# Fourteen of the dot products by GpSimd and ScalarE, more dots ahead of the gates, sixteen V rows added inside U

## The reference

```
h = rmsnorm(x) @ w_in                # 1024 x 2400
x = x + concat(four kinds of attention over h) @ w_out
x = x + peer(rmsnorm(x))
```

```
act = gelu(einsum('td,thkd->thk', h, u_tab[idx]))
out = einsum('thk,thkd->td', gate * act, v_tab[idx])   # gate: softmax of the 16 best scores
```

## Time and profile before

| | |
|---|---|
| median of 3 runs | 1641.34 us (1639.16 to 1643.42) |
| profiled execution | 1639.23 us, its span 1637.4 us |
| TensorE busy | 1593.9 us (97%) |
| VectorE busy | 1065.6 us (65%) |
| ScalarE busy | 543.6 us (33%) |
| GpSimd busy | 686.8 us (42%) |
| DMA | 525.77 MB, mean 321 GB/s |

### The profile page before, as it was taken

How to read it: one execution, slowest core, us unless ns; L and a number is a source line. 1 busy time by engine, 2 the same in 40 slices (tenths; PEclk the granted TensorE clock), 3 DMA queues, 4 the chain that set the end, 5 groups by cost and what they waited for, 6 DMA issues and landing times.

```text
span 1637.4 us, 31846 instructions
## 1 busy us (share of the span) xinstructions
PE 1593.9 (97%) x11548; PEld 1547.6 (95%) x11548; DVE 1065.6 (65%) x2517; ACT 543.6 (33%) x1424; POOL 686.8 (42%) x556
## 2 busy tenths in 40 slices
PE   7999999999999899999999999999999999999998
PEld 6888999999999899999988889999999999999998
DVE  4784799688886643343357847896888866544443
ACT  5775522655553000000056755216555540000000
POOL 6516614555553432233256156144545535333331
PEclk9999999999999999999999999999999999999999
DMA  9026288999999999999930262798999999999996
GB/s 356 14 100 248 91 302 330 338 410 410 409 409 361 389 410 408 408 407 408 407 135 1 104 257 91 282 336 313 411 409 409 409 372 380 410 410 409 409 410 272
DMA packets 141942, 525.77 MB, mean 321 GB/s; under 512 B 16160, under 2 KB 19744, under 8 KB 139424
## 3 DMA queue, kind: packets, MB, share of 16 engines
q1 hardware_dynamic: 86336, 322.57, 50.5%
q0 software_dynamic: 55520, 202.14, 31.5%
HBM read 523.60 MB, written 1.05 MB: 320 GB/s over the span
## 4 chain that ended last, share of the span: by engine, by line
PE 82%; DMA 10%; DVE 3%; ACT 2%; issue 1%; POOL 1%; SPq 0%; DVEq 0%; ACTq 0%; POOLq 0%
PE ps L617 81%; DMA ring<-in_peer_v 6%; DMA nat<-in_peer_v 3%; PE ps L614 2%; ACT grid L297 0%; DVE grid L1400 0%; DVE negmax L1404 0%; DMA x<-in_x 0%; ACT grid L969 0%; DVE x L1458 0%; ACT grid L1068 0%; ACT wh L1005 0%; POOL wl L586 0%; DVE grid L1453 0%; ACT grid L955 0%
## 5 line engine op out<-in xcount | busy, mean ns | idle before, releaser
L617 PE MATMUL ps<-grid,ring 128*128 128x160 f32 (+1 forms) x3712 | 525.6, 300 | 11.2 <-DMA ring<-in_peer_v 10.2
L617 PE MATMUL ps<-grid,nat 128*128 128x160 f32 (+1 forms) x3712 | 526.0, 300 | 6.4 <-DMA nat<-in_peer_v 4.9
L617 PEld LDWEIGHTS ps<-grid,ring 128*128 128x128 f32 x3712 | 508.9, 190 | 16.5 <-issue 16.3
L617 PEld LDWEIGHTS ps<-grid,nat 128*128 128x128 f32 x3712 | 508.9, 190 | 12.4 <-issue 12.0
L1682 DVE SCALAR_TENSOR_TENSOR grid<-grid,amount 128x1024 f32<-128x1024 f32 x96 | 123.3, 1285 | 157.6 <-DMA grid<-in_peer_v,lists 156.8
L1682 DVE SCALAR_TENSOR_TENSOR grid<-gath_a,amount,grid 128x1024 f32<-128x1024 f32 x94 | 120.7, 1285 | 141.4 <-DMA gath_a<-in_peer_v,lists 140.0
L599 POOL DMA_INDIRECT gath_a<-in_u_rows,lists x96 | 130.8, 1363 | 178.8 <-DVE dots L1651 124.0
L599 POOL DMA_INDIRECT gath_a<-in_peer_v,lists x96 | 107.5, 1120 | 224.4 <-PE ps L617 122.3
L579 POOL TENSOR_TENSOR wl<-grid,wh 128x512 fp32r<-128x512 f32 (+2 forms) x128 | 142.6, 1141 | 118.7 <-ACT wh L1005 97.0
L599 POOL DMA_INDIRECT grid<-in_peer_v,lists x96 | 101.9, 1062 | 186.1 <-PE ps L617 121.9
L1005 ACT ACTIVATE wh<-grid 128x512 fp32r<-128x512 f32 (+2 forms) x128 | 68.0, 575 | 336.9 <-PE ps L617 336.7
(11 more groups left out here) (198 smaller groups left out, 1764.9 us busy)
## 6 DMA issues: line engine op xcount, KB each, us to landing
nat<-in_peer_v SPq DMA_DIRECT2D x128, 512.0 KB
ring<-in_peer_v SPq DMA_DIRECT2D x128, 512.0 KB
nat<-in_peer_u SPq DMA_DIRECT2D x104, 512.0 KB
ring<-in_peer_u SPq DMA_DIRECT2D x104, 512.0 KB
grid<-in_peer_u SPq DMA_DIRECT2D x48, 512.0 KB, 5.8
grid<-in_peer_wq SPq DMA_DIRECT2D x8, 2048.0 KB, 9.8
grid<-in_w_out SPq DMA_DIRECT2D x2, 4096.0 KB, 13.9
grid<-in_w_in SPq DMA_DIRECT2D x3, 2048.0 KB, 15.8
```

The source lines that it names most:

```text
L617: return nc.tensor.matmul(dst, a, b, start=first, stop=last)
```

## The change

GpSimd multiplies the first 14 gathered rows of U by `xs` (into the buffer itself), and ScalarE sums each by an activation with `accum_out`, behind the gelus of blocks 20, 21, 23, 24, 26, ... 40. VectorE starts with dot 14. `EARLY_DOTS` goes from 24 to 36, so VectorE does 22 dots ahead of the gates: ten after all of the routing (where the steps had ten dots between them), and twelve after the first `hots`. The dots end with group 29. Sixteen rows of V are added in groups 32 to 39, `weigh` stands in group 32, and ScalarE forms `acts` two turns (16 blocks) before the end of U. `FREE_ROWS` goes from 12 to 26. `turn_lists` moves from block 44 to 40, its copies on ScalarE with it, and the Exp from gelu 31 to gelu 27. The buffers get a semaphore each, `gath_free`.

```diff
-EARLY_DOTS = 24
+EARLY_DOTS = 36
+POOL_DOTS = 14
+SUM_BEHIND = tuple(20 + 8 * n // 5 for n in range(POOL_DOTS))
-FREE_ROWS, LAST_ROW_AT = 12, 118
+FREE_ROWS, LAST_ROW_AT = 26, 118
...
 # GpSimd
                     def gather(m):
-                        if m >= OCT:
-                            pool.wait_ge(gath_used, past[gath_used] + m - OCT + 1)
+                        if m >= NR + OCT:
+                            pool.wait_ge(rows_added, past[rows_added] + m - NR - OCT + 1)
+                        elif m >= OCT:
+                            pool.wait_ge(gath_free[m % OCT], past[gath_free[m % OCT]] + m // OCT)
...
-                    for m in range(2 * NR):
+                    for m in range(OCT):
+                        gather(m)
+                    for n in range(POOL_DOTS):
+                        b = n % OCT
+                        pool.wait_ge(gath_in[b], past[gath_in[b]] + 16 * (n // OCT + 1))
+                        nc.gpsimd.tensor_tensor(gath[b], gath[b], xs, ALU.mult).then_inc(multiplied, 1)
+                        if n:
+                            gather(OCT + n - 1)
+                    for m in range(OCT + POOL_DOTS - 1, 2 * NR):
...
 # TensorE
-                        if b == NA - 4:
+                        if b == NA - 8:
                             turn_lists()
...
 # ScalarE (the loops over early_oct before are replaced)
+                    for b in range(NA):
+                        gelu(b // OCT, b % OCT)
+                        if b == 27:
+                            act.wait_ge(best_shift, past[best_shift] + 1)
+                            A(best[:, :, :], best[:, :, :], ACT.Exp).then_inc(wexp_ready, 1)
+                            A(lamt[:, 6:7], ones[:, :], ACT.Gelu_apprx_tanh)
+                        if b in SUM_BEHIND:
+                            n = SUM_BEHIND.index(b)
+                            act.wait_ge(multiplied, past[multiplied] + n + 1)
+                            A(gath[n % OCT], gath[n % OCT], ACT.Copy, accum_out=dots[:, n:n + 1]).then_inc(gath_free[n % OCT], 1)
+                        if 36 <= b < 36 + NB // OCT:
+                            A(late[:, b - 36, :], over(ones[:, 0], 1, OCT * DT), ACT.Copy).then_inc(ones_ready, 1)
+                        if b == NA - 8:
+                            act.wait_ge(lists_t, past[lists_t] + 1)
...
+                        if b in (NA - 6, NA - 3):
+                            hot_i(0, (b - NA + 6) // 3)
                     late_oct(QA)
-                    loop(act, QA + 1, NO - 1, late_oct)
+                    loop(act, QA + 1, NO - 2, late_oct)
+                    for free in gath_free:
+                        act.wait_ge(free, past[free] + NR // OCT)
+                    A(acts[:, :], dots[:, :], ACT.Gelu_apprx_tanh).then_inc(acts_ready, 1)
+                    late_oct(NO - 2)
                     late_oct(NO - 1)
-                    act.wait_ge(gath_used, past[gath_used] + NR)
-                    A(acts[:, :], dots[:, :], ACT.Gelu_apprx_tanh).then_inc(acts_ready, 1)
...
 # VectorE: step 65 of the routing now also copies the helpers' tokens
-                            v.scalar_tensor_tensor(out=xs[own, :], ...).then_inc(picked, 1)
+                            ch.step(v.scalar_tensor_tensor(out=xs[own, :], ...))
+                            helped(0).then_inc(picked, 1)
...
-                    for n in (*range(20), *range(31, 39), 64, 65, *range(39, 47), 66, *range(20, 30)):
+                    for n in (*range(20), *range(31, 39), 64, 65):
                         routing(n)
                     dve.wait_ge(picked, past[picked] + 2)
-                    dot(0)
-                    dot(1)
-                    routing(30)
-                    for n in range(47, 63):
+                    left = (*range(20, 31), *range(39, 47), 66, *range(47, 63))
+                    for n in (*left, 63):
                         routing(n)
-                        if n % 2 == 0:
-                            dot(n // 2 - 22)
-                    routing(63)
-                    for n in range(10, 16):
+                    for n in range(POOL_DOTS, POOL_DOTS + 10):
                         dot(n)
...
                     hots(0)
                     hots(1)
-                    for n in range(16, EARLY_DOTS):
+                    for n in range(POOL_DOTS + 10, EARLY_DOTS):
                         dot(n)
...
+                        n = EARLY_DOTS + 2 * m
+                        if m == NG4 - 8:
+                            weigh()
                         for i in range(2):
-                            if EARLY_DOTS + 2 * m < NR:
-                                dot(EARLY_DOTS + 2 * m + i)
+                            if n < NR:
+                                dot(n + i)
+                            elif m >= NG4 - 8:
+                                add_row(2 * (m - NG4 + 8) + i)
                             times_gelu(NA + 2 * m + i, m + 1)
-                    weigh()
-                    for n in range(NR):
+                    for n in range(16, NR):
                         add_row(n)
```

More of the change, by code:

```diff
@@ L309, in build @@
         gath_in = [S(f"gath_in{b}") for b in range(OCT)]
+        gath_free = [S(f"gath_free{b}") for b in range(OCT)]
         dve_chain = S("dve_chain")
@@ L353, in build @@
                 (NK, "prod_done act_stored y_done"),
-                (2 * NR, "gath_used"),
+                (NR, "rows_added"),
+                (POOL_DOTS, "multiplied"),
+                (NR // OCT, " ".join(f"gath_free{b}" for b in range(OCT))),
                 (32 * NR // OCT, " ".join(f"gath_in{b}" for b in range(OCT))),
@@ L1161, in next_hot @@
                         hot_i(g + (s + 2) // 4, (s + 2) % 4)
-                    def early_oct(q):
-                        for s in range(OCT):
-                            gelu(q, s)
                     def late_oct(q):
@@ L1174, in _ @@
                     A(lamt[:, 6:7], ones[:, :], ACT.Gelu_apprx_tanh)
-                    for q in range(QA - 2):
-                        early_oct(q)
-                    act.wait_ge(best_shift, past[best_shift] + 1)
-                    A(best[:, :, :], best[:, :, :], ACT.Exp).then_inc(wexp_ready, 1)
-                    A(lamt[:, 6:7], ones[:, :], ACT.Gelu_apprx_tanh)
-                    for s in range(OCT):
-                        gelu(QA - 2, s)
-                        if s >= 4:
-                            A(late[:, s - 4, :], over(ones[:, 0], 1, OCT * DT), ACT.Copy).then_inc(ones_ready, 1)
-                    for s in range(OCT):
-                        gelu(QA - 1, s)
-                        if s < 6:
-                            A(late[:, 4 + s, :], over(ones[:, 0], 1, OCT * DT), ACT.Copy).then_inc(ones_ready, 1)
-                        if s == 3:
+                    for b in range(NA):
[11 more added lines that the diff above has]
+                        if b == NA - 8:
                             act.wait_ge(lists_t, past[lists_t] + 1)
@@ L1651, in dot @@
                         v.tensor_tensor_reduce(out=gath[b], in0=gath[b], in1=xs, scale=1.0, scalar=0.0,
-                                               op0=ALU.mult, op1=ALU.add, accum_out=dots[:, n:n + 1]).then_inc(gath_used, 1)
+                                               op0=ALU.mult, op1=ALU.add, accum_out=dots[:, n:n + 1]).then_inc(gath_free[b], 1)
                     def weigh():
```

32 lines of the change are left out of this document (16 added, 16 removed).

## The result

| | median of the runs | lowest to highest | profiled span | mean clock |
|---|---|---|---|---|
| before | 1640.72 us (5 runs) | 1639.16 to 1643.42 | 1637.4 us | 0.999 |
| after | 1675.74 us (5 runs) | 1674.19 to 1676.39 | 1672.4 us | 0.985 |

The ratio is 1.0212, 95% interval 1.0201 to 1.0223: 35 us slower. The forecast was 1649 with a range of 1632 to 1668. The direction is right, the size is not, and the range doesn't hold it.

A forecast was written before the change was run, and what follows sets the result against it. TensorE, busy 1593.9 of 1637.4 us, was taken as the main bound, with V waiting for DMA. Two stalls of 15.5 us less 23 of relief gave +8 on 1639.2, 1647.2; the median 2.1 above: 1649, range 1632 to 1668.

The forecast's parts named there:

- point 1: In V, fewer gathers per block cut DMA waits: layer 0 gains 19 us, layer 1 4.2, together 23.
- The check by layer: Alternative count by layer: layer 0, bound by bytes for most of its span, at -3.5 us, layer 1 at +11.3.
- the room in DMA at 275 to 300 us is used less: In U, Pool issues 13 gathers between 261 and 305 us, where before it issued 16 by 302.
- point 2: In U, times_gates(0) waits for dots 14 to 35, so TensorE stalls after product 52: 12.8 us before Pool and VectorE interference.
- S: TensorE's stall ahead of gates(2) after product 52, per layer: 12.8 + 2.7 = 15.5 us, upper bound 27.
- cover of 18 us, just enough: VectorE's lists_ready at 299 us, TensorE needing it for turn_lists ahead of block 40 at 299.1.
- the second rival: Pool's products, held up by VectorE, end at 320 us and stop TensorE: S = 27, +31, 1672 us; chance 0.12.
- point 3: Pool's products and VectorE's two-input operations block each other: 3.6 us more for Pool, decode slowed, lists_ready 299 instead of 281.
- The rest costs nothing: ScalarE's sums (some 18 us), rows added in U and weigh fit into existing slack; no time added.

The follow-up runs named there:

- e7: Kernel before with only EARLY_DOTS 24 to 36, so 36 dots stand ahead of the gates; no products, no rows moved: 1680.7 us, ratio 1.0245.
- e4: Kernel before with only 8 rows of V added in U (FREE_ROWS 20, weigh four turns before the loop's end): 1638.0 us, ratio 0.9988.
- e11: Kernel before with 36 dots ahead of the gates, all on VectorE in its old order, and 16 rows of V in U: 1658.2 us, ratio 1.0113.
- e13: Kernel after with eight turns of SyncE's loop over U's late blocks written out, same transfers, waits and order: 1671.5 us, ratio 1.0185.
- e3: Kernel after with turn_lists and the copies behind it back at block 44 instead of 40: 1669.1 us, ratio 1.0177.
- e9: Kernel after with VectorE's order of before behind picked, a decode first and the picks behind it: 1660.6 us, ratio 1.0128.
- e6: Kernel after with gathers 21 to 35 fetching 64 of 128 partitions, the other half left out: 1676.0 us, ratio 1.0209.
- e1: Kernel after with 24 dots instead of 36 ahead of the gates, and 8 rows of V in U, not 16: 1664.7 us, ratio 1.0153.
- e2: Kernel after with GpSimd's 14 products left out of the computation, same waits, gathers and sums: 1666.4 us, ratio 1.0165.
- e5: Kernel after with U's blocks 36 to 43 asked for eight products later: 1679.8 us, ratio 1.0232.
- e14: Kernel before with 8 rows of V in U, five of six next-layer w_in chunks asked for behind V, and FREE_ROWS 10: 1613.9 us, ratio 0.9835.
- e8: Kernel before with 8 rows of V in U and the last three of six next-layer w_in chunks asked for behind V: 1631.3 us, ratio 0.9944.

## Why the prediction was wrong, step by step

*V is relieved (point 1): the size right, the meaning wrong in layer 0.* V takes 286.1 and 278.4 us where 283.6 and 278.2 were forecast. But the 18.5 us of layer 0 are not a term of their own. That layer ends with its bytes, and V was shorter since DMA had run ahead while TensorE stood in U. It takes both the rows and the stop: V in layer 0 takes 304.8 us with the stop alone (e7), 298.7 with 8 rows alone (e4) and 286.1 with 16 rows and the stop (e11). The check by layer at the end of the sum said "layer 0, bound by bytes for most of its span, comes out at -3.5", and this was the right way to count. Done in full it would have asked where the change leaves DMA unused: 10.6 us more than before, of which 3.6 at 275 to 300, 3.6 at 300 to 325, 1.3 at 250 to 275 and 0.9 at the turn to V. Layer 0 came out at +10.0. The prediction saw that "the room in DMA at 275 to 300 us is used less", and gave it no price in layer 0. In layer 1, where w_in is not loaded, V's 4.1 us are a gain as forecast.

*The gates start later (point 2): the step that failed.* The term is S = 15.5 per layer; U came out 26.9 and 29.2 us longer. The forecast let the 15 missing gathers start at 305, as GpSimd's product 13 was to end at 303.7, landed gather 35 at 340.8, and put 2.7 us on top for the time that GpSimd and VectorE cost each other. The transfer was about right: 35.8 us forecast, 38.7 measured (314.1 to 352.8). The start was wrong, by 9 us, and so gates(2) came 142.2 us after block 0 instead of 133.4.

Two things that the forecast had at nothing make the start late, and each hides the other. First, TensorE stopped for 4.9 us at 254 to 260, which no row of before foretold. It held gelu 20, the first sum behind it and gather 8 by 5.73 us, and product 13 ended at 311.2 (forecast 303.7, or 307.3 with VectorE in the way). Second, lists_ready came at 307.8 against "cover of 18 us, just enough", and the forecast took that to be free. It held TensorE and gelu 40, and with them sum 13 and gather 21. In after the second adds only 1.00 us to the first. With the stop gone and the lists late (e13), gather 21 waits 6.67 us and comes at 313.45. With the stop there and the lists out of the way (e3) it comes at 311.35. Only with both gone (e9) does it come at 307.35, and gates(2) 5.3 us earlier in layer 0 and 7.6 in layer 1. The two halves of the second chain both stood in the prediction, one in the second rival ("ScalarE, which waits for it behind gelu 40, holds gelu 41") and one in point 3. They were not joined in this direction. What the dots alone do was forecast well (e7: 135.6 us). What makes TensorE stop at 254 us stays open.

*Pool and VectorE (point 3): the mechanism right, the sizes nearly.* GpSimd's products take 2.36 to 2.50 us and were hardly held up. All of the waiting is VectorE's: 16.4 us in three decode groups where 18 were forecast. The lists were late by the rest. VectorE came to the decode at 260.1 and not at 252, mostly since a copy of 128x16 took 2.82 us and the picks stood 4.5 us. In e13 it comes at 253.2 and all three groups run beside products, 48 us for 27, and lists_ready is at 305.9 all the same. The Trainium skill, "SBUF — State Buffer", section "Who interferes with whom", has the one that comes second wait for the whole instruction, and names copies and casts beside operations of two inputs. The trace agrees: the cast at 290.22 takes 2.00 us instead of 0.18, to the end of GpSimd's product at 292.16. The forecast had charged the two-input operations alone.

*"The rest costs nothing": not so.* The slow clock behind each stop was not counted: 2.4 us behind gates(2) in each layer, by the second rule.

*The total.* Forecast 2 x 15.5 - 23 = +8. Measured 26.9 + 29.2 - 18.5 - 4.1 = +33.5 from U and V, and 1.5 us that block 0 starts later. S was 27 and 29, just the 27 of the second rival (1672, with a chance of 0.12), but not by its way: the products were not slowed to end at 320, they ended at 311.2, and product 13's sum waited for TensorE and not TensorE for it. That V's relief came out at 22.6 of 23 us is partly luck, as layer 0's part was made by the stop.

## What to carry to other kernels

Where one stage after another is full of DMA, a stage's own bytes don't price a change: count what the change leaves unused of the DMA, from the first stretch with room to the end of the last full one. A forecast that something is ready just in time has to be followed to everything that stands behind it on the other engines, here list, transposes, gelu, sum, buffer, gather. And a stop ahead of a later wait costs little as long as the later wait is for something else: e13 took 4.9 us away in layer 0 and the like in layer 1, and the time fell by 4 in all. When two delays overlap, test them alone and together.

## What was not expected of the hardware

- A gather of 64 of 128 partitions took nearly the DMA time of a whole one (e6: share 1.03 at 242 GB/s over 325 to 350 us, where after has 409).
- TensorE, ScalarE and VectorE stopped together at 250 to 257 us in after, e1, e2, e3, e5 and e6, ScalarE for 7.63 to 8.35 us, for nothing that the profile names beyond "issue" and "remote". There is no such stop of TensorE in before, e4 and e7 to e14; ScalarE alone shows one of about 4 us in before (layer 1), e4, e7 and e8. After, e5 and e6 have smaller stops of TensorE for "issue" at 328 to 334 us too. Writing out a loop on SyncE took the stop at 254 us away (e13). That instructions arrive late while gathers fill the DMA queues is a guess that no run shows, and what decides whether a program has the stop stays open.
- Once TensorE's 12 us stop ended, gates(2) took 2.08 us instead of 1.05 and the two blocks behind it 5.98 instead of 4.51, and 350 to 375 us had a clock of 0.79.
